# A 32-byte tile of padding that moves every later tile of a float32 transformer kernel from byte 32 to byte 0 of a 64-byte stretch

## The chip, the core and the metric

The kernel is one program on one core of one Trainium2 chip. It is written by hand, engine by engine, with semaphores: TensorE (PE) multiplies, VectorE (DVE), ScalarE (ACT) and GpSimd (POOL) prepare operands and finish results, and SyncE (SP) issues the DMAs. The metric is the device time of one execution in microseconds (us), the median of several.

## The reference, cut to what matters

Three transformer layers run on a sequence of 512 tokens of width 1024, in float32. Layers 1 and 2 are: feed forward, mixer, feed forward. Layer 3 is: mixer, feed forward. The five feed forwards are

```
def swiglu(h, w_gate, w_up, w_down):
    return (jax.nn.silu(h @ w_gate) * (h @ w_up)) @ w_down      # 1024 -> 2816 -> 1024
x = x + 0.5 * swiglu(rmsnorm(x, norm), w_gate, w_up, w_down)    # layers 1 and 2; without the 0.5 in layer 3
```

The mixers of layers 1 and 2 project to pooled channels and to q, k and v, rotate a part of q and k, run three dilated windows of attention on 12 heads, and project back. The mixer of layer 3 is a spatial gating group beside an attention group with compressed, selected and windowed keys. Nothing of this is touched by the change.

## The kernel before

**Precision.** A float32 product is done as three matmuls in the reduced format `float32r`. Each operand is split into a high part, rounded to `float32r`, and a low part, what is left. The product is high times high, low times high and high times low. So nearly all matmuls come in threes (lines 771 to 773 and 862 to 864), and every weight tile and every activation tile has a high and a low version in SBUF.

**Two operands.** A matmul has a stationary operand, which a separate weight load puts into the array (PEld in the profile), and a moving operand, which streams through it. The row of a matmul in the profile names the moving tile first and the stationary one second, and the shape that it gives (128x512) is that of the moving one. In the product stages the moving operand is a weight tile (`wh`, `wl` or `wx`) and the stationary one an activation tile (`ea` or `ss`). Everywhere else the moving one is the activation (`act_all`, `xh`, `xl`, `mh`, `ml`, 512 tokens) and the stationary one 128 columns of `wh` or `wl`.

**Stages.** A feed forward has a product stage and a down stage. The product stage computes gate and up in six chunks of columns, with seven half-size block products in place of eight (a Strassen-like scheme whose operand sums VectorE forms). Five chunks have 512 moving columns and the last 256. Each of its quarters of work is 12 matmuls: two row blocks, two token blocks, three matmuls each. The weights of a quarter are split by ScalarE (line 1454, high) and VectorE (line 2036, low) into one of three slots in turn, two of them in `wh` and `wl` and the third in `wx` (`high_slot` and `low_slot`). The down stage multiplies the 22 tiles of `act_all` with 22 weight tiles for each of 8 output tiles; these weights are split by GpSimd (lines 726 and 729) from `raw` into `wh` and `wl`, and so are those of the mixers.

**Order.** The order on each engine is the order of the code, and semaphores alone tie the engines together. The change adds or moves no instruction.

**SBUF.** Tiles are declared one after the other, and each takes a multiple of 32 bytes per partition. First come the tiles that live through the whole program: `x`, `raw`, `wh`, `wl`, `sq`, `rstd`, `ident`, `ones`, all of which begin at a multiple of 64 bytes, and after them the small ones (`gains` to `nrc`, 544 bytes in all). Then come the tiles of the layers, which share one region between them by stage (`block1`, `gate`, `down`, `mix1`, `mix2`). Because of the 544 bytes this region begins at byte 77,472, which is 32 past a multiple of 64, and so does every large tile in it: `ea`, `ss`, `wx`, `rawa`, `act_all`, `xh`, `xl`, `mh1`, `ml1`, `qs`, `ks`, `kl`, `sc`, `pt`, `pmid`, `plow`, `xg`, `sf` and those of `mix2`. The sizes of the large tiles, and nearly all offsets used within them, are multiples of 64. This document calls a tile that begins at a multiple of 64 **even** and one that begins 32 past it **odd**.

The three slots of weights are these:

```
def high_slot(slot):
    return wx[:, 0, :] if slot == 2 else wh[:, slot, :, :].rearrange("p k n -> p (k n)")
def low_slot(slot):
    return wx[:, 1, :] if slot == 2 else wl[:, slot, :, :].rearrange("p k n -> p (k n)")
```

Of the kernel before, what the change touches and what calls it, by code (L numbers as in the profile page):

```python
# [36 lines left out]
P = 128  # L37
# [177 lines left out]
def build(nc, d):  # L215

    ctx = ExitStack()
    with ctx:
# [3 lines left out]
        def sb(name, shape, dt=F32, at=ctx):  # L222
            return at.enter_context(nc.sbuf_tensor(name, shape, dt))
# [16 lines left out]
        fin4 = sb("fin4", [P, NQ])  # L240
        rc = sb("rc", [P, NQ])
        nrc = sb("nrc", [P, NQ])


        block1 = ExitStack()
# [2592 lines left out]
```

How the kernel before makes its waits and increments, by code:

```python
            def load_unit(u):  # L582
                if u in DOWN_AT or u - 1 in DOWN_AT or u - 2 in DOWN_AT or u - 3 in DOWN_AT:
                    n = next(n for n in range(FFNS) if 0 <= u - DOWN_AT[n] < 4)
                    sp.wait_ge(gu_lo, product_end(n, LAST - 1, 3 if u % 4 >= 2 else 6))
                else:
                    sp.wait_ge(split_done, u - 3)
                sp.dma_start(raw[:, u % 4, :], d["stream"][u]).then_inc(raw_in[u % 4], 16)
# [13 lines left out]
            def first_chunk(n):  # L602
                if n in (1, 3):
                    sp.wait_ge(ml_done, (n // 2) * 8 + 9)
                if n == 2:
                    sp.wait_ge(unit_used, DOWN_AT[1] + 20 + 3)
                if n == 4:
                    sp.wait_ge(mh2_done, 8)
                for role in ("b11", "b12", "b22"):
                    load_quarter(n, 0, role)
                sp.wait_ge(split_done, DOWN_AT[n] - (2 if n == 2 else 0))
                load_quarter(n, 0, "b21")
# [1 line left out]
            def next_chunk(n, c):  # L615
                for role, i in (("b11", 3), ("b12", 4), ("b21", 5), ("b22", 6)):
                    sp.wait_ge(gu_lo, product_end(n, c - 1, i))
                    load_quarter(n, c, role)
# [1 line left out]
            def last_chunk(n):  # L621
                sp.wait_ge(gu_lo, product_end(n, LAST - 1, 4))
                sp.dma_start(rawa[:, 1, :, :], d["gu_last"][n][:, 0:2, :]).then_inc(gu_in[1], 16)
                sp.wait_ge(t_sum, summed(n, LAST - 1, 3, 1))
```

## Time and profile before

| | |
|---|---|
| time, median of 3 runs | 2618.0 us (2617.86 to 2619.72) |
| the profiled execution's own time | 2618.17 us |
| its span, first to last instruction | 2616.4 us |
| PE busy | 2498.6 us (95%), 12216 matmuls |
| DVE busy | 1645.9 us (63%) |
| ACT busy | 1096.2 us (42%) |
| POOL busy | 726.1 us (28%) |
| mean granted TensorE clock | 0.987 |

The product stages of the five feed forwards begin at about 12, 624, 993, 1598 and 2236 us and last some 235 us each, the down stages at 261, 861, 1234, 1834 and 2475 us for some 130 us each. The mixers of the three layers lie at 403, 1376 and 1977 us. The busy time of a matmul in the profile is longer than the distance to the next one, since they are pipelined: what a matmul costs is the distance between the starts of two neighbours.

### The profile page before, as it was taken

What the parts mean: (1) busy time and instruction counts of PE and PEld (TensorE: products, weight loads), DVE (VectorE), ACT (ScalarE), POOL (GpSimd) and SP (SyncE); (2) the same over time, 40 slices, a digit from 0 to 9 for tenths busy, and PEclk for the clock granted to TensorE, in tenths of its full rate; (3) what the DMA queues carried; (4) which work ended last, traced back from release to release, by engine and by line L of the source; (5) the groups of instructions that cost most, each with busy time, mean ns of one, the idle gap of its engine ahead of it and who ended that gap; (6) DMA issues with size and microseconds to landing.
All of it is one profiled execution on the core that took longest, in us unless ns stands there. A gap on an engine that the chain in (4) does not pass through costs nothing.

```text
span 2616.4 us, 31330 instructions
## 1 busy us (share of the span) xinstructions
PE 2498.6 (95%) x12216; PEld 2016.4 (77%) x12216; DVE 1645.9 (63%) x2066; ACT 1096.2 (42%) x1720; POOL 726.1 (28%) x426
## 2 busy tenths in 40 slices
PE   6998999999999998998999999998999988999898
PEld 5887787777887786887877777887787866788787
DVE  8886427668887327887227668887226656988612
ACT  5554103565554214554114655554212564655410
POOL 1001566523000460001566432000564322000164
PEclk9999999999999999999999999999999999999999
DMA  4332222112331223222222113332223111232222
GB/s 152 114 112 73 81 97 76 54 41 97 113 129 65 73 73 129 98 96 81 83 95 73 57 45 117 114 119 73 76 94 137 49 41 65 81 113 81 81 89 73
DMA packets 51667, 229.49 MB, mean 88 GB/s; under 512 B 7104, under 2 KB 10048, under 8 KB 37696
## 3 DMA queue, kind: packets, MB, share of 16 engines
q1 hardware_dynamic: 49808, 225.66, 24.8%
q8 instruction: 98, 1.61, 0.2%
q10 hardware_dynamic: 1712, 1.82, 0.2%
q14 instruction: 49, 0.40, 0.1%
HBM read 225.36 MB, written 2.10 MB: 87 GB/s over the span
## 4 chain that ended last, share of the span: by engine, by line
PE 87%; DVE 8%; issue 2%; ACT 2%; DMA 1%; POOL 0%; SPq 0%; DVEq 0%; ACTq 0%; POOLq 0%
PE bank L771 12%; PE bank L773 12%; PE bank L772 12%; PE bank L862 12%; PE bank L863 12%; PE bank L864 12%; PE bank L881 2%; PE bank L972 2%; PE bank L957 2%; PE bank L941 1%; DVE wl L2036 1%; PE bank L788 1%; PE bank L942 1%; PE bank L1194 1%; DVE rawa L2024 1%
## 5 line engine op out<-in xcount | busy, mean ns | idle before, releaser
L726 POOL TENSOR_SCALAR wh<-raw 128x1024 fp32r<-128x1024 f32 x192 | 210.8, 1098 | 1846.8 <-PE bank L864 1196.7
L729 POOL TENSOR_TENSOR wl<-raw,wh 128x1024 fp32r<-128x1024 f32 x192 | 469.9, 2448 | 16.0
L771 PE MATMUL bank<-act_all,wh 128*128 128x512 f32 (+1 forms) x902 | 356.9, 396 | 0.0
L773 PE MATMUL bank<-act_all,wl 128*128 128x512 f32 (+1 forms) x902 | 351.3, 389 | 0.0
L772 PE MATMUL bank<-act_all,wh 128*128 128x512 f32 (+1 forms) x902 | 350.9, 389 | 0.0
L1974 DVE SCALAR_TENSOR_TENSOR x<-bank,x 128x512 f32<-128x512 f32 x63 | 43.4, 690 | 443.4 <-PE bank L773 443.4
L1454 ACT ACTIVATE wh<-rawa 128x1024 fp32r<-128x1024 f32 x155 | 164.4, 1062 | 218.5 <-PE bank L864 186.8
L862 PE MATMUL bank<-wh,ss 128*128 128x512 f32 (+1 forms) x660 | 249.2, 378 | 3.6 <-DVE wl L2036 3.5
L863 PE MATMUL bank<-wh,ss 128*128 128x512 f32 (+1 forms) x660 | 247.3, 375 | 0.0
L864 PE MATMUL bank<-wl,ss 128*128 128x512 f32 (+1 forms) x660 | 247.2, 375 | 0.0
L2036 DVE TENSOR_TENSOR wl<-rawa,wh 128x1024 fp32r<-128x1024 f32 x155 | 189.3, 1223 | 82.5 <-ACT wh L1454 82.5
L773 PEld LDWEIGHTS bank<-act_all,wl 128*128 128x128 f32 x902 | 169.1, 187 | 39.2
L772 PEld LDWEIGHTS bank<-act_all,wh 128*128 128x128 f32 x902 | 169.4, 188 | 36.5
L771 PEld LDWEIGHTS bank<-act_all,wh 128*128 128x128 f32 x902 | 169.3, 188 | 36.4
L862 PE MATMUL bank<-wh,ea 128*128 128x512 f32 (+1 forms) x464 | 180.1, 388 | 1.6 <-issue 1.6
L863 PE MATMUL bank<-wh,ea 128*128 128x512 f32 (+1 forms) x464 | 178.4, 384 | 0.0
L864 PE MATMUL bank<-wl,ea 128*128 128x512 f32 (+1 forms) x464 | 177.8, 383 | 0.0
L771 PE MATMUL bank<-xh,wh 128*128 128x512 f32 x416 | 166.0, 399 | 0.0
L772 PE MATMUL bank<-xl,wh 128*128 128x512 f32 x416 | 164.2, 395 | 0.0
L773 PE MATMUL bank<-xh,wl 128*128 128x512 f32 x416 | 164.2, 395 | 0.0
L1454 ACT ACTIVATE wh<-raw 128x1024 fp32r<-128x1024 f32 x101 | 107.1, 1061 | 118.6 <-PE bank L864 113.0
L862 PEld LDWEIGHTS bank<-wh,ss 128*128 128x128 f32 x660 | 124.0, 188 | 32.7 <-DVE wl L2036 5.9
(351 smaller groups left out, 5274.3 us busy)
## 6 DMA issues: line engine op xcount, KB each, us to landing
raw<-in_stream SPq DMA_DIRECT2D x192, 512.0 KB, 3.2
rawa<-in_gu SPq DMA_DIRECT2D x65, 1024.0 KB, 4.8
raw<-in_gu SPq DMA_DIRECT2D x35, 1024.0 KB, 4.7
rawa<-in_gu_last SPq DMA_DIRECT2D x5, 1024.0 KB, 5.2
rawa<-in_gu_last SPq DMA_DIRECT2D x10, 512.0 KB, 4.8
x<-in_x SPq DMA_DIRECT2D x8, 256.0 KB, 8.3
w1k<-in_w1k SPq DMA_DIRECT2D x1, 2048.0 KB, 8.9
w1v_low<-in_w1v SPq DMA_DIRECT2D x1, 1024.0 KB, 5.4
```

The costliest lines, as they stand in the source:

```text
L726: nc.gpsimd.tensor_scalar(wh[:, h % 2, :, :], src, 1.0, 1.0, ALU.mult, ALU.mult)\
L729: nc.gpsimd.tensor_tensor(wl[:, h % 2, :, :], src, wh[:, h % 2, :, :].bitcast(F32), ALU.subtract).then_inc(split_done, 1)
L771: mm = nc.tensor.matmul(bank, wh[:, slot, k, :], rh, start=start, stop=False)
L772: mm = nc.tensor.matmul(bank, wh[:, slot, k, :], rl, start=False, stop=False)
L773: return nc.tensor.matmul(bank, wl[:, slot, k, :], rh, start=False, stop=stop)
L862: nc.tensor.matmul(o, sh, wh_[:, r], start=first, stop=False, skip_group_check=True)
L863: nc.tensor.matmul(o, sl, wh_[:, r], start=False, stop=False, skip_group_check=True)
L864: mm = nc.tensor.matmul(o, sh, wl_[:, r], start=False, stop=final, skip_group_check=True)
L881: tr = nc.tensor.transpose(B[6 + f % 2][:, t * P:(t + 1) * P], product_rows(c)[:, t, (f % 4) * P:(f % 4) * P + P], ident[:, :])
L957: tr = nc.tensor.transpose(B[(3, 4)[g % 2]][:, kt * P:(kt + 1) * P], sc[:, g % 3, kt * P:(kt + 1) * P], ident[:, :])
L1454: nc.scalar.activation(high_slot(slot), buffered(c, OPERAND[i], half), ACT.Copy).then_inc(gu_hi, 1)
L2036: V.tensor_tensor(low_slot(slot), buffered(c, OPERAND[i], half), high_slot(slot).bitcast(F32), ALU.subtract)\
```

## The change

An unused tile of 8 float32, 32 bytes per partition, is declared behind the small tiles. All tiles declared after it move up by 32 bytes, so that each odd one becomes even. The tiles before it stay. No instruction reads or writes the new tile, and the instructions of every engine are the same and in the same order; only addresses differ. A few small tiles inside the region that were even become odd (`sden`, `srec`, `seen0`, `cmin`, `cden`, `gss`, `gate_stack`), and so do the views of `padded` and `win` that begin 8 elements into them.

```
         fin4 = sb("fin4", [P, NQ])
         rc = sb("rc", [P, NQ])
         nrc = sb("nrc", [P, NQ])
+        room = sb("room", [P, 8])
```

## Rows read from the trace of the kernel before

**Rows 1.** The page: chain that ended last, by engine

```profile
PE 87%; DVE 8%; issue 2%; ACT 2%; DMA 1%; POOL 0%; SPq 0%; DVEq 0%; ACTq 0%; POOLq 0%
```

**Rows 2.** Busy us (instructions) of each engine by stretch

```profile
261.00:391.00 130.00, 129.12 (x581) 104.09 (x580) 44.23 (x50) 18.08 (x30) 74.19 (x44) 1.00 0.27 88
402.00:625.00 223.00, 222.74 (x1167) 173.34 (x1166) 153.24 (x248) 114.62 (x231) 105.54 (x60) 1.00 0.21 71
624.00:648.00 24.00, 21.36 (x95) 16.55 (x93) 22.72 (x25) 16.87 (x20) 0.00 (x0) 1.00 0.00 0
650.00:690.00 40.00, 40.00 (x173) 32.11 (x172) 36.24 (x36) 21.82 (x25) 0.00 (x0) 1.00 0.36 129
690.00:730.00 40.00, 40.00 (x174) 32.37 (x173) 33.67 (x34) 20.53 (x24) 0.00 (x0) 1.00 0.30 106
```

**Rows 3.** Matmul groups by form, 512 columns: xcount, busy us, mean ns

```profile
L772 PE MATMUL bank<-act_all,wh 128*128 128x512 f32 x858 | 338.7, 395 | 0.0
...
L863 PE MATMUL bank<-wh,ss 128*128 128x512 f32 x540 | 213.6, 396 | 0.0
...
L773 PE MATMUL bank<-xh,wl 128*128 128x512 f32 x416 | 164.2, 395 | 0.0
...
L863 PE MATMUL bank<-wh,ea 128*128 128x512 f32 x384 | 153.3, 399 | 0.0
...
L863 PE MATMUL bank<-wx,ss 128*128 128x512 f32 x260 | 101.9, 392 | 0.0
...
L863 PE MATMUL bank<-wx,ea 128*128 128x512 f32 x216 | 86.5, 401 | 0.0
...
L773 PE MATMUL bank<-mh,wl 128*128 128x512 f32 x192 | 75.8, 395 | 0.0
```

**Rows 4.** Timeline on TensorE in a product stage: start us, us one took

```profile
696.39 0.39 PE L862 MATMUL bank<-wx,ss 128*128 128x512 f32 x1
...
699.13 0.40 PE L862 MATMUL bank<-wh,ss 128*128 128x512 f32 x1
...
701.93 0.40 PE L862 MATMUL bank<-wh,ea 128*128 128x512 f32 x1
...
706.12 0.39 PE L862 MATMUL bank<-wx,ea 128*128 128x512 f32 x1
...
707.48 0.40 PE L862 MATMUL bank<-wh,ea 128*128 128x512 f32 x1
```

**Rows 5.** Timeline in a down stage, first and 27th of a run

```profile
300.29 0.40 PE L771 MATMUL bank<-act_all,wh 128*128 128x512 f32 x1
...
306.36 0.40 PE L773 MATMUL bank<-act_all,wl 128*128 128x512 f32 x1
```

**Rows 6.** Groups on TensorE by form, 256 columns

```profile
L864 PE MATMUL bank<-wl,ss 128*128 128x256 f32 x120 | 33.6, 280 | 0.0
...
L864 PE MATMUL bank<-wl,ea 128*128 128x256 f32 x80 | 24.6, 308 | 0.0
...
L772 PE MATMUL bank<-act_all,wh 128*128 128x256 f32 x44 | 12.3, 279 | 0.0
...
L864 PE MATMUL bank<-wx,ss 128*128 128x256 f32 x40 | 11.3, 282 | 0.0
```

**Rows 7.** Groups on TensorE by form, plain float32 operands

```profile
L972 PE MATMUL bank<-pt,vtok 128*64 128x256 f32 x192 | 23.4, 385 | 0.0
L972 PE MATMUL bank<-sq,vtok 128*64 128x256 f32 x192 | 23.4, 385 | 0.0
```

**Rows 8.** Groups on VectorE by form, the low halves

```profile
L2036 DVE TENSOR_TENSOR wl<-raw,wh 128x1024 fp32r<-128x1024 f32 x101 | 123.6, 1224 | 40.5 <-ACT wh L1454 40.2
L2036 DVE TENSOR_TENSOR wx<-rawa,wx 128x1024 fp32r<-128x1024 f32 x80 | 98.0, 1225 | 25.8 <-ACT wx L1454 25.8
```

**Rows 9.** Groups on ScalarE by form, the high halves

```profile
L1454 ACT ACTIVATE wh<-raw 128x1024 fp32r<-128x1024 f32 x101 | 107.1, 1061 | 118.6 <-PE bank L864 113.0 <-PE bank L773 5.6
L1454 ACT ACTIVATE wx<-rawa 128x1024 fp32r<-128x1024 f32 x80 | 84.9, 1061 | 98.9 <-PE bank L864 95.6 <-DMA rawa<-in_gu 3.2
```

More of the change, by code:

```diff
@@ L242, in build @@
         nrc = sb("nrc", [P, NQ])
+        room = sb("room", [P, 8])
         block1 = ExitStack()
```

## The prediction, made before the changed kernel ran

> **What bounds the kernel now.** I read the chain of waits first, then the busy times by stretch, then the groups by form, then the timeline of TensorE. The chain lies on TensorE for 87% [rows 1]. The stretches say where it does not [rows 2]. In the down stage (261 to 391) TensorE is busy 129.1 of 130 us, in the mixer (402 to 625) 222.7 of 223, and in the middle of a product stage (650 to 690, 690 to 730) all the time. Only the head of a product stage (624 to 648) is another's: VectorE is busy 22.7 of 24 us there, and TensorE gets 95 matmuls through. So the end is set by the distance from one matmul to the next, nearly everywhere. The granted clock is 1.00 in all these stretches, the 2.4 GHz level.
>
> **What the change can touch.** No instruction is added, removed or moved, and no wait. Only the start addresses of the tiles in the shared region move, from odd to even. So the only terms are durations that depend on an address. I look for pairs in the trace that do the same work on tiles of different parity.
>
> VectorE and ScalarE: the low half from even tiles takes 1224 ns, from odd tiles 1225 [rows 8]; the high half takes 1061 ns in both cases [rows 9]. These are their largest forms. I cost both engines at nothing. If 1 ns were real, VectorE's 2066 instructions would make 2 us off the path. GpSimd's two big forms read `raw` and write `wh` and `wl`, which stay where they are: nothing. The few GpSimd and VectorE operations on views that turn odd are small and off the path: nothing, at most 1 us either way.
>
> TensorE, long forms. Here the trace has a pair. The product stage uses `wx` as moving operand for every third quarter and `wh`/`wl` for the others, with the same stationary tiles. With `wx` both operands are odd; with `wh` the moving one is even and the stationary one odd. The timeline gives the distance [rows 4]. The 12 matmuls of a `wx` quarter from 696.39 to 699.13 take 2.74 us, 228.3 ns each; the 12 of the `wh` quarter behind it, to 701.93, take 2.80 us, 233.3 ns each. The `wx` quarter isn't uniform: of the one that begins at 704.73 (12 matmuls, the next quarter begins at 707.48) the last six, from 706.12, take 1.36 us, 226.7 ns each, and its first six 1.39 us, 231.7 ns each. It looks as if a run of equal parity starts at the pace of the quarter before it and settles. The groups by form agree: 396 ns against 392 for line 863 with `ss` [rows 3]. With `ea` they don't (399 against 401), but the `ea` groups hold the first quarters of each feed forward, where TensorE waits; I don't use them.
>
> The down stage has the pair turned round: the moving `act_all` is odd, the stationary `wh`/`wl` even. From 300.29 to 306.36 lie 26 distances in 6.07 us, 233.5 ns each [rows 5]. So one odd and one even costs 233.4 ns whichever is which, and odd with odd 226.7 when settled. The difference, 6.7 ns at 2.4 GHz, is 16 columns, and 16 float32 are 64 bytes. That fits a cost by the parity of the two streams against each other. It does not fit a cost of being odd, since two odd ones are the fastest. This is my reading and not shown: `wx` also lies elsewhere than `wh`.
>
> After the change all pairs are even with even. The trace has no long `float32r` pair of that kind. I take it to behave as odd with odd does.
>
> **The sum.** Mixed matmuls of 512 columns by the groups, three lines each [rows 3]: down stages 3 x 858 = 2574, product stages 3 x (540 + 384) = 2772, mixers 3 x (416 + 192) = 1824, together 7170. Of these some lie in the heads of the product stages, where VectorE sets the pace: 95 of a stage's 1008 matmuls, so about 50 mixed ones in each of five, 250 in all. That leaves 6920. The price of one lies between 4 ns (the means 396 and 392) and 6.6 (233.3 less 226.7, settled). I take 5.8, nearer to the settled end, because there will be no mixed quarter left to start from: 6920 x 5.8 = 40 us. The `wx` matmuls, 3 x (260 + 216) = 1428, gain where they now start slowly: half of them, less those in the heads, 650 x 5.0 = 3 us. The ends of these two are 28 to 46 and 0 to 3.
>
> Short forms, 256 columns [rows 6]: line 864 takes 280 ns with `wl,ss` and 282 with `wx,ss`, so equal parity costs 2 ns more there; 3 x (120 + 80 + 44) = 732 of them, 1.5 us lost. (The 308 with `ea` holds waits.) Matmuls on plain float32 show no difference: 385 ns with odd `pt` against odd `vtok` and with even `sq` against odd `vtok` [rows 7]. I cost them at nothing.
>
> What comes next. In the middle of a product stage VectorE is busy 33.7 to 36.2 of 40 us [rows 2]. A TensorE faster by 2.5% needs 39 us for the same work, so VectorE stays below it, but closely, and where its order is uneven some of the gain comes back as waits for the low half (line 2036). In the down stage GpSimd is busy 74.2 of 130 us and doesn't limit. The mixer has VectorE at 153 of 223. I take off 4 us for new waits (ends 0 and 12). The sum is 40 + 3 - 1.5 - 4, about 38 us. Against the profiled execution's own 2618.17 us (span 2616.4, 1.8 us around it, and 0.2 above the median of the runs, 2618.0) that is 2580 us. With the ends it is 2618 - 49 = 2569 to 2618 - 14 = 2604.
>
> A rule of the Trainium skill speaks against all this. "TensorE: Matmul & The Clock Gate", in its section "Step-by-step: what each phase is for", says that TensorE has two independent read ports into SBUF and that loading the next weights takes no read bandwidth from the running matmul; "SBUF — State Buffer", section "Specifications (TRN2)", gives lines of 16 bytes, and an odd tile here is already at a multiple of 16. By these two an address 32 bytes further on changes nothing, and the time would be 2618. The 233.3 and 226.7 ns of rows 4 aren't explained by them, though they don't refute them either, since `wx` differs in place too.
>
> **Rivals.**
>
> *Place, not parity: no change.* `wh` and `wl` lie in the first 66 KB of the partition and all odd tiles behind 77 KB. Every mixed pair is also a pair of one low and one high tile, and every odd pair is high with high. If the place makes the pace, nothing moves: 2618, with the 1 us of small views either way 2617 to 2619. For it: rows 7 show no parity effect on plain float32, and the short forms go the other way [rows 6]. Against it: the pace is the same 233.4 whether `wh` is moving with `ss` or stationary with `act_all`, whose 90 KB reach from 90 to 180 KB [rows 4, 5], so place would have to mean just "the low one of the two". The page's rule ends at the same number. Chance 0.24.
>
> *Equal parity is the dear one: slower.* The weight load of the next matmul and the moving read of this one both walk through 64-byte stretches. With equal parity they meet on the same half. The short forms show that price, 2 ns, since there the load isn't hidden; `wx` is fast for its place. Then all mixed ones pay it: (7170 + 732) x 2 = 16 us, 2634. It decides from the point where an even and even pair is slower than 233.3 ns. Against it: at `wx` the long form is faster by 5 ns with equal parity. Chance 0.12.
>
> *More than parity: even starts save on their own.* If an odd start also costs each long read one 64-byte stretch more, even with even is faster than odd with odd by up to another 6.7 ns. On some 8300 long matmuls that is 56 us, of which VectorE in the product stages would let through about half there (a pace 5% faster needs 38 of 40 us against VectorE's 36.2): some 45 us, 2535. For it: 233.3 and 226.7 both lie above the 213.3 ns that 512 columns take at 2.4 GHz. Against it: with one operand even already there is no sign of a gain. Chance 0.14.
>
> **How the numbers follow.** Parity as read has 0.50 and gives 2580, its own range 2569 to 2604. With the third rival, 0.14 at 2535, that makes 0.64 for faster by over 0.2% (5.2 us, about what a measurement of this kernel can tell from no change). No change has 0.24, slower 0.12. The likeliest case gives the predicted time, 2580. The range reaches from 2538, which leaves out the far half of the third rival, to 2621, which takes in no change and leaves out slower: about 0.19 lies outside.
>
> **What would show it.** Right: in the profile after, 12 matmuls of a `wh` quarter take 2.72 us instead of 2.80, and 26 distances of a down stage 5.90 us instead of 6.07. The means of lines 771 to 773 and 862 to 864 at 512 columns fall from 395 or 396 to 389 or 390 everywhere, `wx` quarters no longer begin slowly, the down stage shortens by about 528 x 6 ns = 3.2 us and the mixer by 3 to 4. VectorE, ScalarE and GpSimd keep their durations to 1 ns or so. The waits of line 862 for line 2036 grow a little. Wrong: the pace stays at 233.3 with `wh` and 228.3 with `wx` (place); it rises above 233.3 (the dear one); it falls below 225 (more than parity). Wrong in size: TensorE faster by the step, but idle before line 862 in the product stages by more than 12 us in all.

## The result: 2603.1 us after, 2617.9 before

The changed kernel takes 2603.09 us (median of 4, 2600.53 to 2604.66), the kernel before 2617.93 beside it (2617.65 to 2619.72). The ratio is 0.9941, its 95% interval 0.9924 to 0.9958: faster by 14.8 us. The forecast was 38 us. The sign, the engine and the effect of addresses were right, the size was not; the time lies in the range of 2538 to 2621, near its slow end.

The profiled execution takes 2600.53 us, its span is 2598.7 us, 17.7 less than before. The page after, first the busy times of the engines and then the chain of waits by engine (before: 87% on PE [rows 1]):

```profile
PE 2480.8 (95%) x12216; PEld 2014.4 (78%) x12216; DVE 1649.8 (63%) x2066; ACT 1095.5 (42%) x1720; POOL 726.2 (28%) x426
...
PE 86%; DVE 9%; issue 2%; ACT 2%; DMA 1%; POOL 0%; SPq 0%; DVEq 0%; ACTq 0%; POOLq 0%
```

PE is busy for 17.8 us less with the same 12216 matmuls; the other engines changed by 4 us or less. The gain is TensorE's. (1.3 of the 17.7 us are none of the change's: the first matmul starts at 10.36 us in this profile, at 11.67 before, and at 12.0 in another profile of the changed kernel.) The question is where. I read it from the distance between the first matmul of a stage and the first of the next. A down stage is counted up to the first matmul of lines 771 to 773 with `xh` (772 to 774 in the kernel after), so three of the five hold the 48 matmuls with which the mixer behind them begins:

| us, sum over the stages | before | after | difference |
|---|---|---|---|
| 5 product stages | 1204.6 | 1204.5 | -0.1 |
| 5 down stages | 697.9 | 687.6 | -10.4 |
| 3 mixers | 702.2 | 696.3 | -5.9 |

The product stages, which have 2772 of the 7170 matmuls that the forecast counted, gained nothing. The timeline of TensorE after says the same matmul by matmul. Its columns are the start and the duration, both in us. First a down stage, 27 distances between these two starts (before: 26 in 6.07 us [rows 5]):

```profile
300.11 0.39 PE L772 MATMUL bank<-act_all,wh 128*128 128x512 f32 x1
...
306.29 0.39 PE L772 MATMUL bank<-act_all,wh 128*128 128x512 f32 x1
```

6.18 us for 27 distances are 228.9 ns each; it was 233.5. Now the middle of a product stage, the first matmul of three quarters in a row, 12 matmuls apart (before: 2.74 us for `wx` and 2.80 for `wh` [rows 4]):

```profile
690.32 0.39 PE L863 MATMUL bank<-wx,ss 128*128 128x512 f32 x1
...
693.06 0.39 PE L863 MATMUL bank<-wh,ss 128*128 128x512 f32 x1
...
695.86 0.39 PE L863 MATMUL bank<-wh,ea 128*128 128x512 f32 x1
```

Again 2.74 us for the `wx` quarter and 2.80 for the `wh` quarter, 228.3 and 233.3 ns: nothing moved. Both operands are even here now, and the pace is that of even with odd. The groups of TensorE by form (count, then busy time in us and the mean in ns) mislead at this point [rows 3, 6]:

```profile
L773 PE MATMUL bank<-act_all,wh 128*128 128x512 f32 x858 | 334.9, 390 | 0.0
...
L864 PE MATMUL bank<-wh,ss 128*128 128x512 f32 x540 | 212.8, 394 | 0.0
...
L774 PE MATMUL bank<-xh,wl 128*128 128x512 f32 x416 | 163.6, 393 | 0.0
...
L865 PE MATMUL bank<-wl,ss 128*128 128x256 f32 x120 | 33.3, 277 | 0.0
```

`act_all,wh` fell from 395 to 390 ns and its mean distance by 4.2 (233.2 to 229.0); that fits. But `wh,ss` fell from 396 to 394 while its distance stayed at 233.3, and `xh,wl` fell by 2 while its distance fell by 3.3. The mean busy time of a matmul follows the pace only roughly, and 2 ns in it prove nothing. The Trainium skill says why a matmul's end can't be trusted ("Perfetto Trace Analysis", section "Tensor Engine Instruction (MATMUL, LD_WEIGHTS)": the end is computed from the instruction's size and a delay for SBUF, and not observed); the two `wh,ss` numbers agree with it.

### The profile page after: what moved, and what is told of

Its sections match the earlier page's. It is cut to its first block, busy times and chain, and to the rows that moved or that the text cites. A ratio compares the mean times of both kernels' runs of the same rounds, so it can differ in the third digit from the quotient of the medians.

```text
span 2598.7 us, 31330 instructions
## 1 busy us (share of the span) xinstructions
PE 2480.8 (95%) x12216; PEld 2014.4 (78%) x12216; DVE 1649.8 (63%) x2066; ACT 1095.5 (42%) x1720; POOL 726.2 (28%) x426
## 4 chain that ended last, share of the span: by engine, by line
PE 86%; DVE 9%; issue 2%; ACT 2%; DMA 1%; POOL 0%; SPq 0%; DVEq 0%; ACTq 0%; POOLq 0%
PE bank L863 12%; PE bank L772 12%; PE bank L864 12%; PE bank L865 12%; PE bank L774 12%; PE bank L773 12%; PE bank L882 2%; PE bank L973 2%; PE bank L958 2%; PE bank L942 1%; DVE wl L2037 1%; PE bank L943 1%; PE bank L789 1%; PE bank L1195 1%; DVE wx L2037 1%
## 5 line engine op out<-in xcount | busy, mean ns | idle before, releaser
L1455 ACT ACTIVATE wh<-rawa 128x1024 fp32r<-128x1024 f32 x155 | 164.3, 1061 | 218.6 <-PE bank L865 187.3
L1455 ACT ACTIVATE wh<-raw 128x1024 fp32r<-128x1024 f32 x101 | 107.1, 1060 | 118.9 <-PE bank L865 113.6
L2037 DVE TENSOR_TENSOR wl<-raw,wh 128x1024 fp32r<-128x1024 f32 x101 | 123.5, 1223 | 40.5 <-ACT wh L1455 40.2
```

What stands on the lines that cost most here:

```text
L1455: nc.scalar.activation(high_slot(slot), buffered(c, OPERAND[i], half), ACT.Copy).then_inc(gu_hi, 1)
L2037: V.tensor_tensor(low_slot(slot), buffered(c, OPERAND[i], half), high_slot(slot).bitcast(F32), ALU.subtract)\
```

## The experiments

**Theories.** After the result these stood: *parity*, as forecast, with something else that hides the product stage's gain; *moving parity*, that the parity of the moving operand alone counts; *order*, that the product stage's sequence of high and low tiles, or how far the low one lies behind the high one, matters. After the first four runs *distance* came in: that the pace depends on how far apart the two operands start, and not on where either lies. "Distance" below always means the start of the moving tile less the start of the stationary one, modulo 256 bytes.

**Parity by itself.** A kernel in which TensorE alone multiplies tiles of zeros (nothing of the reference is computed): 48 matmuls of 512 columns for each pair of tiles, in the down stage's order of high and low and in the product stage's, with four distances between high and low of the moving tile and two of the stationary one. `_o` tiles lie behind a gap of 32 bytes.

```
for j in range(16): mm(bank, sta_e[hi j], mov_e[hi]); mm(bank, sta_e[hi j], mov_e[lo]); mm(bank, sta_e[lo j], mov_e[hi])
```

> TensorE alone, nothing else runs: 64 groups of 48 long float32r matmuls on zeros, each group with another moving tile (mov_e even, mov_o odd), stationary tile (sta_e, sta_o), order of high and low (D as in the down stage, P as in the product stage), and distance of the low part behind the high one. It computes none of the reference and writes zeros. Equal parity is the fast one (as predicted): every e,e and o,o group has about 227 to 229 ns per matmul (mean duration 389 to 391), every e,o and o,e group 233.3 (396). Parity of the moving operand alone, in the order D (what the changed kernel's down stage shows): groups with mov_e 229, with mov_o 233.3 whatever the stationary tile; in the order P no difference. Distance of the low part (wx has 4096 bytes, wh 8192): groups differ by the distance and not by the parity.

The timeline of TensorE in it, one row for each run of 48 (start, then duration of the run):

```profile
32.82 11.05 PE L43 MATMUL bank<-mov_e,sta_e 128*128 128x512 f32 x48
43.71 11.36 PE L45 MATMUL bank<-mov_e,sta_o 128*128 128x512 f32 x48
54.91 11.36 PE L47 MATMUL bank<-mov_o,sta_e 128*128 128x512 f32 x48
66.11 11.08 PE L49 MATMUL bank<-mov_o,sta_o 128*128 128x512 f32 x48
77.03 11.07 PE L51 MATMUL bank<-mov_e,sta_e 128*128 128x512 f32 x48
```

From start to start 10.89, 11.20, 11.20 and 10.92 us: 226.9, 233.3, 233.3 and 227.5 ns (226.7 for the fourth too once its first ten are left out). All 16 combinations of order and inner distances give these same values. Even with even is as fast as odd with odd, the order of high and low means nothing, and no other engine is needed. So the first of the three expectations came out, parity alone would have given the forecast, and the kernel did not follow it. But all tiles here had been a multiple of 256 bytes apart, or that and 32.

**Half the shift on the other side.** Two kernels move `wh` and all behind it by 32 bytes, without and with the tile of the change.

```
+        room_w = sb("room_w", [P, 8])     # ahead of wh: both kernels
+        room = sb("room", [P, 8])         # behind nrc: the second only
```

> The 32 bytes stand ahead of wh, so wh, wl, sq are odd and the shared region is even, as in the changed kernel. Equal parity theory: every down and mixer matmul is mixed again (moving even, stationary odd), 233.3 ns, total 2618 us. Moving parity theory: act_all and xh stay even, the down stage stays at 229.0 ns per matmul, total 2601 to 2605 us.

> 32 bytes ahead of wh and 32 behind nrc: wh and wl odd and the region odd too. Equal parity theory: down stage 229.0 ns, total about 2603 us. Moving parity theory: act_all and xh are odd, 233.3 ns, total 2618 us.

Measured 2616.29 and 2603.74 us (one run each; the kernel before 2620.54 beside them). In the first, all large tiles have changed parity and the distances are those of before; in the second, `wh` is odd and the region odd again, and the distances are those of after. The group `act_all,wh` of the first kernel (count, busy us, mean ns):

```profile
L773 PE MATMUL bank<-act_all,wh 128*128 128x512 f32 x858 | 338.7, 395 | 0.0
```

And the same group of the second:

```profile
L774 PE MATMUL bank<-act_all,wh 128*128 128x512 f32 x858 | 334.8, 390 | 0.0
```

338.7 us at 395 ns is what before had, to the digit [rows 3]; 334.8 at 390 is what after has (334.9). The measured pace is 233.2 ns in the down stage of the first and 229.0 in that of the second. So the moving operand's parity alone doesn't count: `act_all` is even in the first and slow, odd in the second and fast. Equal parity is not refuted by these two; it asks for the same two times, and so does distance. (2616.29 and the 2620.54 beside it are one run each; over all its runs the kernel before lies between 2616.6 and 2620.7.)

**A further 32 bytes.** The unused tile has 64 bytes, so the region is odd again.

```
-        room = sb("room", [P, 8])
+        room = sb("room", [P, 16])
```

> The padding is 64 bytes instead of 32, so the region is odd again but 64 bytes from where it was. If only the address modulo 64 counts: all as before, 233.3 ns in the down stage, 2618 us. If the address modulo 128 or more counts (the gain came from the shift as such): the down stage differs from 233.3 ns and the total from 2618 by 5 us or more.

2621.32 us (one run). The distances are 96 and 160, and the pace is 233.4 ns in the down stage and 234.0 at `wh` in the product stage. By parity it should be the time of before, and it is (2620.5 beside it), and the pace with `xh` in the mixers is 233.4 (233.1 before). This run alone leaves a period of 64 bytes open, if something hides the gain of the product stages.

**128 bytes from each other, and none.** Tiles of 96 and of 224 bytes, beside the change itself once more.

```
+        room = sb("room", [P, 24])        # room96; room224: [P, 56]; room32_again: [P, 8]
```

> The padding is 96 bytes, so the region is even again, and it now begins at a multiple of 128 bytes as wh does (in the changed kernel it begins 64 past one). Theory A, the distance between the two operands modulo 128 counts (0: 226.7 ns, 64: 229.0 in the down stage and 233.3 in the product stage, 32 and 96: 233.3 and more): the down stage falls to 226.7 ns per matmul, wh quarters of the product stage to 226.7 to 228, and the total to 2570 to 2580 us. Theory B, parity modulo 64 alone, and the product stage is held by something else: the same as the changed kernel, 229.0 and 233.3 ns, 2603 us.

> The changed kernel once more, on the same chip as room96: 2600 to 2605 us by every theory.

> The padding is 224 bytes, so the region begins at the same place modulo 128 as with 96 bytes, but 128 bytes further. If distance modulo 128 is all that counts: same as room96 to 0.2%, same ns per matmul. If modulo 256 counts too: another pace in the down or the product stage.

The change again: 2602.21 us (5 runs), ratio 0.9933 (0.9920 to 0.9947), as in the result. 96 bytes: 2613.21 us (9 runs), ratio 0.9978 (0.9969 to 0.9988), pace 232.3 in the down stage and 233.1 in the product stage. 224 bytes: 2578.93 us. At that size both distances are 0, and the pace is 226.8 to 227.0 everywhere in the product and down stages. The changed kernel and these two have the same parities and paces of 229.0, 232.3 and 226.8 ns in the down stage, which rules out a period of 64 bytes. A period of 128 bytes, which the expectation of the 96 byte kernel had at 2570 to 2580 us, is ruled out too: the kernels with 96 and 224 bytes differ by 128 bytes alone and take 2613.21 and 2578.93 us.

**The whole table.** TensorE alone again, eight moving and eight stationary tiles, each 32 bytes further on than the one before (modulo 256), all 64 pairs. The first row of it, `mov_a` with `sta_a` to `sta_h`, goes through the distances 0, 224, 192, 160, 128, 96, 64 and 32.

```
mov_a ... mov_h, sta_a ... sta_h: start of the n-th = 32 * n bytes modulo 256
```

> TensorE alone on zeros, nothing of the reference is computed: 64 groups of 48 long float32r matmuls, moving tiles mov_a to mov_h and stationary tiles sta_a to sta_h, each letter 32 bytes further on modulo 256 (a is at 128, e at 0), in the order of the down stage, and 8 groups with mov_a in the order of the product stage. Theory A (distance modulo 128): a with a or e 226.7 ns, a with c or g slower than that (229 or 233.3), a with b, d, f, h 233.3; the same for each other letter by its distance. Theory B (modulo 64): c and g are as fast as a and e, 226.7.

The timeline of that row (start, duration of the run, 48 matmuls each; the last line, which gives the end of the eighth run, is cut off by the window):

```profile
46.48 11.05 PE L84 MATMUL bank<-mov_a,sta_a 128*128 128x512 f32 x48
57.37 11.35 PE L86 MATMUL bank<-mov_a,sta_b 128*128 128x512 f32 x48
68.56 11.36 PE L88 MATMUL bank<-mov_a,sta_c 128*128 128x512 f32 x48
79.76 11.40 PE L90 MATMUL bank<-mov_a,sta_d 128*128 128x512 f32 x48
91.00 11.32 PE L92 MATMUL bank<-mov_a,sta_e 128*128 128x512 f32 x48
102.16 11.37 PE L94 MATMUL bank<-mov_a,sta_f 128*128 128x512 f32 x48
113.36 11.16 PE L96 MATMUL bank<-mov_a,sta_g 128*128 128x512 f32 x48
124.36 11.36 PE L98 MATMUL bank<-mov_a,sta_h 128*128 128x512 f32 x48
135.55 9.73 PE L100 MATMUL bank<-mov_b,sta_a 128*128 128x512 f32 x41
```

The starts lie 10.89, 11.19, 11.20, 11.24, 11.16, 11.20, 11.00 and 11.19 us apart. The mean over all pairs of a distance, without the first ten of each run:

| distance, bytes modulo 256 | 0 | 32 | 64 | 96 | 128 | 160 | 192 | 224 |
|---|---|---|---|---|---|---|---|---|
| ns per matmul of 512 columns | 226.7 | 233.3 | 228.9 | 233.3 | 232.5 | 234.4 | 233.4 | 233.4 |

The other 56 pairs fall on the same eight values by their distance, to 0.2 ns but for one with 128 (233.2), and so do eight runs in the product stage's order with `mov_a`. Both theories of the expectation are refuted: 0 and 128 differ by 5.8 ns (period 128), 0 and 64 by 2.2 (period 64). It is not symmetric: the moving tile 64 bytes ahead is nearly the fast case, and 64 behind (192) is not. This is the asymmetry that split the change: the down stage and the mixers, with the activation moving, went from distance 32 to 64; the product stages, with `wh` moving, from 224 to 192.

**The best version, timed, and the same distances at odd addresses.** The second kernel has 32 bytes ahead of `wh` and 224 behind `nrc`, so all large tiles begin 32 past a multiple of 64.

```
+        room_w = sb("room_w", [P, 8])     # ahead of wh: odd_aligned only
+        room = sb("room", [P, 56])        # behind nrc: both
```

> 224 bytes of padding once more, timed. The distance between moving and stationary operand is a multiple of 256 bytes for all big pairs. Distance theory: 226.7 to 227 ns per long matmul in all stages, 2575 to 2583 us, ratio to before 0.985 +- 0.002. If the single run of 2578.9 was luck: 2600 or more.

> 32 bytes ahead of wh and 224 behind nrc: wh, wl and every large tile behind them begin 32 past a multiple of 64, and all at the same place modulo 256. Distance theory: only the distance counts, so the same as with 224 bytes alone: 226.7 to 227 ns per long matmul, 2575 to 2583 us. If a start at a multiple of 64 bytes is worth something in itself: slower than room224_timed by more than 5 us.

2578.67 us (4 runs, 2578.06 to 2579.87), ratio 0.9852 (0.9838 to 0.9865), and 2577.99 us (5 runs), ratio 0.9849 (0.9835 to 0.9862): the same within their spread. The multiple of 64 bytes, which the change was made to reach, is worth nothing by itself; the distance is worth 39.5 us. Both beat the kernel before and the changed one. Three quarters of a product stage in the timeline of the 224 byte version (start, duration):

```profile
691.95 0.39 PE L863 MATMUL bank<-wh,ea 128*128 128x512 f32 x1
...
694.67 0.39 PE L863 MATMUL bank<-wx,ea 128*128 128x512 f32 x1
...
697.39 0.39 PE L863 MATMUL bank<-wh,ea 128*128 128x512 f32 x1
```

2.72 us for the `wx` and for the `wh` quarter, 226.7 ns in both. The waits of TensorE on VectorE's low halves in it (us, count, longest):

```profile
PE bank L863 <- DVE wx L2037: 16.6, 6, 11.7
...
PE bank L863 <- DVE wl L2037: 3.4, 7, 1.6
```

The same two rows of the waits in the kernel before:

```profile
PE bank L862 <- DVE wx L2036: 17.0, 6, 11.7
...
PE bank L862 <- DVE wl L2036: 3.5, 8, 1.6
```

16.6 and 3.4 us against 17.0 and 3.5: the faster TensorE didn't run into VectorE. Against before the product stages are shorter by 16.9 us, the down stages by 15.7, the mixers by 5.7; the sum, 38.3, is the span's difference of 2616.4 to 2578.1.

**The mixers.** Their 5.7 us look like the 5.9 of the change itself, as if distance 0 gave them nothing more than 64. Taken one by one they differ. Those of layers 1 and 2 take 221.8 us each before, 219.9 after and 219.1 with 224 bytes, to 0.1 in every profile of these distances. Layer 3's moves from profile to profile at the same distances: 256.5, 257.3 and 258.7 us at distance 64, and 254.9, 258.2 and 258.2 at 0 (258.6 before). The granted clock in it does too. In the two kernels with 224 bytes, the same 70 us of that mixer (stretch, length, busy time and count on PE, PEld, DVE, ACT and POOL, then the mean granted clock, DMA share and GB/s), first in `room224`, then in `room224_timed`:

```profile
2113.80:2183.80 70.00, 59.23 (x360) 46.50 (x361) 44.32 (x90) 37.73 (x89) 14.03 (x8) 0.93 0.16 61
```

```profile
2112.00:2182.00 70.00, 58.64 (x345) 46.45 (x346) 41.33 (x88) 36.39 (x87) 11.50 (x7) 0.88 0.16 61
```

15 matmuls fewer in the same time; the clock stands at 0.50, the 1.2 GHz level, for 10.2 us of the first mixer and 17.0 of the second, and the mixer takes 254.9 and 258.2 us. So the mixers' sum in one profile says little to 3 us. The mean gain over the three profiles each is 4.9 us at distance 64 and 6.8 at 0.

That is still less than 1824 matmuls at 6.5 ns would give, and the timeline of `room224_timed` shows why. A run of 84 matmuls from 396.21, and a run of 12 from 419.79, between matmuls of other forms:

```profile
396.21 0.39 PE L772 MATMUL bank<-xh,wh 128*128 128x512 f32 x1
...
415.25 0.39 PE L942 MATMUL bank<-ks,qs 128*128 128x512 f32 x1
...
419.79 0.40 PE L772 MATMUL bank<-xh,wh 128*128 128x512 f32 x1
...
422.55 0.60 PE L958 MATMUL bank<-ident,sc 128*128 128x128 f32 x4
```

19.04 us for 84 are 226.7 ns each, 2.76 us for 12 are 230.0. At distance 0 a run behind other forms begins slowly and settles in about ten matmuls, and most runs with `xh` are of 6 to 12.

**The mirror image.** With 160 bytes the down stage has distance 192 and the product stages 64, the change's two distances exchanged.

```
+        room = sb("room", [P, 40])
```

> 160 bytes of padding: distance modulo 256 is 192 in the down stage and the mixers (act_all or xh less wh) and 64 in the product stage (wh less ss), the reverse of the changed kernel. Distance theory with the table of micro2: down and mixer 233.3 ns as before, wh quarters of the product stage 228.8. The 2520 wh matmuls outside the heads of the product stages gain 4.5 ns each, 11 us, so 2605 to 2611 us; less is lost to waits for VectorE only if the time is nearer to 2618. Parity theory: even region, same as the changed kernel, 2602.

2612.91 us (10 runs, 2609.39 to 2614.31), ratio 0.9977 (0.9968 to 0.9987). The two groups, columns as above:

```profile
L773 PE MATMUL bank<-act_all,wh 128*128 128x512 f32 x858 | 338.6, 395 | 0.0
...
L864 PE MATMUL bank<-wh,ss 128*128 128x512 f32 x540 | 210.4, 390 | 0.0
```

The down stage stays at 395 ns (pace 233.3, 698.0 us in all) and `wh,ss` falls from 396 to 390 (pace 229.6, product stages 7.6 us shorter). Which stage gains is chosen by the sign of the distance. The size missed: 2605 to 2611 us had been expected, from 11 us in the product stages. A part of what is missing is in the `wx` quarters, which keep their distance of 0 and were counted as unchanged:

```profile
693.99 0.40 PE L863 MATMUL bank<-wx,ss 128*128 128x512 f32 x1
...
696.76 0.40 PE L863 MATMUL bank<-wh,ss 128*128 128x512 f32 x1
...
699.52 0.39 PE L863 MATMUL bank<-wh,ea 128*128 128x512 f32 x1
```

2.77 us for the 12 of the `wx` quarter, more than for the `wh` quarter behind it (2.76) and more than the 2.74 of before. By the mean over all, `wx` runs at 231.0 ns here and at 229.0 before.

**Short and plain forms.** TensorE alone: 256 and 128 columns, plain float32, and 512 cut to 480 columns with starts below 32 bytes.

```
for j in range(16): mm(bank[:, 0:256], sta_a[hi j], mov_a[0:256]); ...
```

> TensorE alone on zeros, nothing of the reference is computed: groups of float32r matmuls of 256 and 128 columns and of plain float32 of 512 columns, mov_a against sta_a to sta_h, and groups whose moving operand begins 4 to 64 bytes into mov_a. From the kernel's own short forms I expect 256 columns to be slowest at distance 0 (120 ns) and fastest at 192 (113.5, mov_a with sta_c); plain float32 the same at all distances; a start of 4 to 16 bytes past a multiple of 32 slower than 0 if the reads are made in pieces of 32 bytes, no different if only whole 32-byte steps count.

Its timeline, runs of 48; first 256 columns with distances 0, 224 and 192, then plain float32 with 512 columns:

```profile
46.21 5.91 PE L84 MATMUL bank<-mov_a,sta_a 128*128 128x256 f32 x48
51.96 5.84 PE L86 MATMUL bank<-mov_a,sta_b 128*128 128x256 f32 x48
57.64 5.82 PE L88 MATMUL bank<-mov_a,sta_c 128*128 128x256 f32 x48
...
134.51 20.81 PE L116 MATMUL bank<-mov_a,sta_a 128*128 128x512 f32 x48
155.16 20.76 PE L118 MATMUL bank<-mov_a,sta_b 128*128 128x512 f32 x48
175.76 20.76 PE L120 MATMUL bank<-mov_a,sta_c 128*128 128x512 f32 x48
```

256 columns: 5.75 and 5.68 us for 48; by all eight distances the pace is 120.0 ns at distance 0, 119.9 at 96 and 117.4 to 118.7 elsewhere (the expectation had 113.5 at 192; measured there 117.8, and the fastest is 160). 128 columns take 111.7 ns and plain float32 429.2 ns at every distance (20.65 and 20.60 us for 48 in the rows; the first also holds the change of form). So the effect belongs to the long reduced-format matmuls; the short ones have it weakly and turned round.

All kernels that compute the reference, in one table. The pace is the mean distance of the matmuls of 512 columns at the full granted clock, in ns:

| padding (bytes) | distance down, mixers | distance product | pace down | pace product, `wh` | time, us |
|---|---|---|---|---|---|
| none (before) | 32 | 224 | 233.2 | 233.3 | 2617.9 |
| 32 ahead of `wh` | 32 | 224 | 233.2 | 233.3 | 2616.3 (one run) |
| 32 (after) | 64 | 192 | 229.0 | 233.3 | 2603.1 |
| 32 and 32 ahead of `wh` | 64 | 192 | 229.0 | 233.3 | 2603.7 (one run) |
| 64 | 96 | 160 | 233.4 | 234.0 | 2621.3 (one run) |
| 96 | 128 | 128 | 232.3 | 233.1 | 2613.2 |
| 160 | 192 | 64 | 233.3 | 229.6 | 2612.9 |
| 224 | 0 | 0 | 226.8 | 226.8 | 2578.7 |
| 224 and 32 ahead of `wh` | 0 | 0 | 226.8 | 226.9 | 2578.0 |

Each pace agrees to 0.7 ns with the table of TensorE alone.

## Why the prediction was wrong

**What bounds the kernel.** Right. TensorE's pace sets the end, and a change of 2 to 3% in it comes out in the time nearly whole.

**The other engines at nothing.** Right. VectorE's and ScalarE's largest forms kept their times to 1 ns (1223 and 1060 after, 1224 and 1061 before), and the gains of the stages are covered by TensorE's distances.

**"All pairs are even with even ... I take it to behave as odd with odd does."** This is the step that failed. As a statement on parity it is even true at distance 0 (226.9 and 226.7 ns in the first experiment). What was wrong is to class the pairs of the kernel by parity. The fast pair in the trace, `wx` with `ss`, was not fast for being odd with odd; these tiles lie 57,344 bytes apart, a multiple of 256. The slow ones were not slow for being mixed, but for lying at 32 or 224. After the change the parities are equal and the distances 64 and 192, which cost 228.9 and 233.4. The two numbers of the trace fitted both readings. The addresses needed to tell them apart could be worked out from the sizes of the declared tiles, and I reduced them to one bit, odd or even, before I compared. I had named an untested doubt (`wx` also lies elsewhere) and weighed it as *place*, which was a different question.

**The sum, term by term.** Product stages: (2772 - 250) x 5.8 = 14.6 us and 3 us for `wx` forecast, 0.1 measured. Down stages: 2574 x 5.8 = 14.9 forecast, 10.4 measured (2574 x 4.2 = 10.8, with 233.2 less 229.0). Mixers: 1824 x 5.8 = 10.6 forecast, 5.9 measured (1248 x 3.3 + 576 x 4.0 = 6.4, by the pace, which went from 233.1 to 229.8 ns with `xh` and from 233.2 to 229.2 with `mh`). VectorE's new waits: -4 forecast, none seen. After, TensorE's waits on the low halves are:

```profile
PE bank L863 <- DVE wx L2037: 14.9, 7, 10.4
...
PE bank L863 <- DVE wl L2037: 3.6, 8, 1.6
```

14.9 and 3.6 us against 17.0 and 3.5 before. Short forms: -1.5 forecast; `wl,ss` fell by 3 ns and lost nothing. The measured terms make 16.3 us, the span 17.7 with its earlier start; by the medians the gain is 14.8 us in the result and 16.7 when run again. With the prices of the distances put in, the method gives the result to 2 us.

**The forecast's number was that of another kernel.** 2580 us is what distance 0 gives (2578.7). There the terms come out: 16.9 for the product stages, 15.7 for the down stages. Only the mixers stay at 5.7 in place of 10.6: the price of 5.8 ns leaves out that each of their short runs begins slowly.

**`wx` quarters begin slowly.** The observation was right: in the changed kernel, whose `wh` quarters stayed slow, the start stayed too (2.74 us), and at 224 bytes of padding it is gone. Its reading, that a run starts at the pace of the quarter before it, doesn't hold: with 160 bytes the quarter before has 229.6 ns, and the `wx` quarters run at 231.0, slower than in any other of the kernels. What sets the start is open.

**The rivals.** *Place*: refuted by the change itself, since `act_all`, far up in the partition, with `wh`, far down, went from 233.2 to 229.0 ns by 32 bytes, and `wh` with `ss` runs at 226.8 at distance 0. *Equal parity is the dear one*: wrong for long forms; for 256 columns distance 0 is in fact the slowest, 120.0 against 117.4 to 119.9. No run shows the stretches of 64 bytes that it reasons with. *More than parity*: refuted, all large tiles at odd addresses are as fast (2578.0). None of them was distance, so the 0.26 that I gave the last two went to mechanisms that the long forms don't show. That the time lies in the range, and even at the near end of parity's own, 2604, is luck: a cause that I hadn't listed brought it there.

**The rule on two read ports.** In the runs, the pace of the same matmul with the same weight load goes from 226.7 to 234.4 ns with nothing but the distance changed. The Trainium skill ("TensorE: Matmul & The Clock Gate", section "Step-by-step: what each phase is for") says the two reads have their own ports and the load takes nothing from the running matmul. The measurement decides: for these forms the cost depends on the two starts together. That speaks against two reads that don't touch each other, but no run shows where they would meet. The no change to which the rule led missed the gain, but was nearer than my number (off by 14.8 against 23 us).

## What to carry to other kernels

When a kernel is bound by matmuls with a weight load before each, work out the start of the moving tile less that of the stationary one modulo 256 bytes for each pair of tiles, and try the padding that makes it 0 (for 512 columns of `float32r`; at 480 and 256 columns 0 isn't the best): here 224 unused bytes gave 1.5% (0.9852, 0.9838 to 0.9865), the 32 bytes of "alignment" 0.6%. When two durations in a trace differ, write down all in which their operands differ (here the full addresses) and find a pair that tells the readings apart before one gets a price. And take a matmul's cost from the distance of starts, since the mean busy time moved by 2 ns where the pace didn't.

## What the runs showed of the hardware

- The pace of long `float32r` matmuls depends on the distance of the operands' starts modulo 256 bytes, 226.7 to 234.4 ns at the 2.4 GHz level, and on the sign of it (64: 228.9; 192: 233.4). Why 256 bytes, and whether the two reads meet in the memory or within TensorE, was not tried and stays open. TensorE alone on zeros gives the paces of the whole kernel to 0.7 ns.
- Steps below 32 bytes matter too: 480 columns, once settled, take 216.7, 220.0, 213.3, 216.7, 220.0, 220.0, 213.3 and 218.3 ns with the moving start 0, 4, 8, 16, 24, 32, 48 and 64 bytes on. I have no rule for these, and in this form distance 0 is not the best.
- 256 columns: 117.4 to 120.0 ns, slowest at 0. 128 columns 111.7 and plain float32 429.2 ns at any distance.
- At distance 0 a short run between other forms doesn't reach the settled pace: 230.0 ns in a run of 12, 226.7 in one of 84.
- The granted clock falls to 0.50 (1.2 GHz) in the mixer of layer 3 for a time that changes between profiles of the same distances (10.2 and 17.0 us), and the mixer takes 254.9 and 258.2 us.
